# A depthwise convolution on TensorE: from two 64-column tiles with two taps each to four 32-column tiles with four taps each, the shifted inputs made through device memory

## Chip, cores and metric

The kernel runs on the 8 cores of one Trainium2 chip, the same program on each, with no traffic between cores. Each core takes 2048 tokens (a quarter of one of two sequences of 8192) and the 128 tokens before them (the halo). The metric is the device time of the slowest core in microseconds.

## What is computed

One layer of a decoder block with model width 1024. The change concerns the convolution branch alone:

```python
x = x + 0.5 * swiglu(rmsnorm(x), ffn1)                 # width 2816
h = rmsnorm(x)
glu_a, glu_b, q, k, v, g_conv, g_attn = split(h @ w_in)
u = glu_a * sigmoid(glu_b)                             # (B, S, 1024)
u = causal_depthwise_conv(u, w, b)                     # 31 taps: out[t] = sum_k w[k] * u[t - 30 + k]
conv_out = silu(layernorm(u)) @ w_proj
attn_out = sliding_window_gqa(rope(q), rope(k), v) @ w_o   # window 128, 16 heads, 4 kv heads
x = x + (sigmoid(g_conv) * conv_out + sigmoid(g_attn) * attn_out) @ w_out
x = x + 0.5 * swiglu(rmsnorm(x), ffn2)
out = rmsnorm(x)
```

## The kernel before

Activations lie transposed: 128 channels on the partitions, 8 chunks of channels, and a tile of 512 tokens (NT) in the free dimension. A core works through four such tiles, and each tile goes through the whole layer: feed-forward 1 (`ffn_gu`, `ffn_down`), the mixer, feed-forward 2, the final norm. With the first tile the 128 halo tokens go along as far as k, v and u.

Weights don't stay on the chip. Each tile streams all of them again from device memory: they are stored as float32 and cast to bf16 by DMAs that GpSimd issues. Blocks of 128 x 8 x 256 (512 KB in bf16) go through a ring `wa` of 7 slots (stream SA), those of the down projections, 256 KB each, through a ring `wd` of 7 (stream SD). `Stream.next` hands out the next slot and issues the load of the block five places further on in SA's list. That load waits until TensorE has released its slot. The list is recorded in a first dry build, in the order in which the program asks for blocks.

Waits are made by hand-built helpers: `op` and `dma` look up which semaphores the buffers that are read or written depend on, and the engine waits for them before the instruction. The program's order on each engine is the order of these calls. `dma` also waits for the previous transfer on its own semaphore. On SyncE's queue (SP) there are few transfers: the x tile and the positions in, the output out, the constants.

In the mixer `emit_glu(cc)` projects chunk cc of glu_a and glu_b (16 matmuls, L299), ScalarE takes the sigmoid (L501), and VectorE writes the product u to `uT`, which keeps the last 30 tokens of the tile before in its first 30 columns (L503; L545 moves them up after the convolution). Then VectorE makes the shifted input of the convolution: `RR[cc % 2][g2]`, for each half g2 of the chunk's channels, holds the 64 channels on partitions 0 to 63 (L510) and the same channels one token later on partitions 64 to 127 (L512).

`emit_conv(cc)` then contracts over these 128 rows. The stationary matrix of 128 x 64 holds two diagonals, the weights of taps 2j and 2j + 1, and the moving input is `RR` read from column 2j. Sixteen such matmuls (j) for each of the two halves, 32 of 512 columns, sum up 32 taps (the last is zero), the halves going to PSUM partitions 0 to 63 and 64 to 127 (L522). The diagonals come ready-made as a weight block of 128 x 2048 through the same ring (`("W", cc)`, `w2`). Two matmuls with ones (L540, L542) sum the result and its square over the channels for the layer norm, one chunk later. The order is glu(0), then for each cc: glu(cc + 1), conv(cc). After the eight chunks come the query chunks with rotary embedding, the layer norm's arithmetic beside them, and the attention.

Of the kernel before, what the change touches and what calls it, by code (L numbers as in the profile page):

```python
# [88 lines left out]
def dma(q, dsem, out_ap, in_ap, rd=(), wr=()):  # L89
# [9 lines left out]
    for b in rd:  # L99
        b.r[dsem] = dsem.n  # L100

class Stream:
    def __init__(self, q, slots, bufs, sems, keys, src, live=2):
# [10 lines left out]
    def _issue(self):  # L114
        j = self.issued
        if j >= len(self.keys):
            return
        s = j % self.depth
        dma(self.q, self.sems[s], self.slots[s], self.src(self.keys[j]), wr=(self.bufs[s],))
        self.issued += 1  # L120
# [17 lines left out]
def _build(rec):  # L138
    nc = bass.Bass("TRN2", target_bir_lowering=False)
    dt = nc.dram_tensor  # L140
# [5 lines left out]
    cols_d = dt("cols", [128, 9, 8], F32, kind="ExternalInput").ap()  # L146
    w2_d = dt("w2", [8, 128, 2048], F32, kind="ExternalInput").ap()
    misc_d = dt("misc", [128, 16], F32, kind="ExternalInput").ap()
# [7 lines left out]
    with ExitStack() as es:  # L156
# [27 lines left out]
        wd_s = [mksem(f"s_wd{i}") for i in range(ND)]  # L184
        uT = sb("uT", [128, 8, 30 + NT], BF16); uT_b = [Buf() for _ in range(8)]
        RR = [[sb(f"RR{i}{g}", [128, 30 + NT], BF16) for g in range(2)] for i in range(2)]
        RR_b = [[Buf(indep=True) for g in range(2)] for i in range(2)]
        cT = sb("cT", [128, 8, NT], BF16); cT_b = [Buf() for _ in range(8)]
# [69 lines left out]
        def late_setup():  # L258
            cdma(POOL, "ident", ident[:], ident_d, ident_b)
            cdma(POOL, "pswap", pswap[:], pswap_d, pswap_b)  # L260
            cdma(POOL, "masks", masks[:], masks_d, masks_b)
            op(DVE, lambda: nc.vector.memset(onesz[:], 0.0), wr=(onesz_b,))
            op(DVE, lambda: nc.vector.memset(onesz[:, 0, 0:64], 1.0), wr=(onesz_b,))
            op(DVE, lambda: nc.vector.memset(onesz[:, 1, 64:128], 1.0), wr=(onesz_b,))
            allk = [b_ for g_ in kTz_b for b_ in g_]
            op(DVE, lambda: nc.vector.memset(kTz[:], 0.0), wr=allk)
            op(DVE, lambda: nc.vector.memset(vz[:], 0.0), wr=vz_b)
            op(DVE, lambda: nc.vector.memset(uT[:], 0.0), wr=uT_b)
            for i_ in range(2):
                for g_ in range(2):  # L270
                    op(DVE, lambda i_=i_, g_=g_: nc.vector.memset(RR[i_][g_][:], 0.0), wr=(RR_b[i_][g_],))
            for gp in range(2):
                for i in range(4):
                    op(ACT, lambda gp=gp, i=i: nc.scalar.activation(
                        out=sinkt[:, gp, i * 128:(i + 1) * 128], in_=ident[:], func=AF.Exp,
                        bias=misc[:, 2 + gp * 4 + i:3 + gp * 4 + i], scale=0.0),
                       rd=(ident_b, misc_b), wr=(sinkt_b,))
# [174 lines left out]
        def mixer(tile_idx, base, N, full, do_norm=True):  # L452
# [41 lines left out]
            def emit_glu(cc):  # L494
# [10 lines left out]
                if full:  # L505
                    W_ = 30 + N
                    for g2 in range(2):
                        rr, rrb = RR[cc % 2][g2], RR_b[cc % 2][g2]
                        lo, hi = 64 * g2, 64 * g2 + 64
                        op(DVE, lambda: nc.vector.tensor_copy(out=rr[0:64, 0:W_], in_=uT[lo:hi, cc, 0:W_]),  # L510
                           rd=(uT_b[cc],), wr=(rrb,))
                        op(DVE, lambda: nc.vector.tensor_copy(out=rr[64:128, 0:W_ - 1], in_=uT[lo:hi, cc, 1:W_]),  # L512
                           rd=(uT_b[cc],), wr=(rrb,))

            def emit_conv(cc):
                nonlocal pending
# [238 lines left out]
def _pack_shared(inp):  # L755
# [120 lines left out]
```

How the kernel before makes its waits and increments, by code:

```python
    def wait(self, sem, val):  # L34
        if val <= 0:
            return
        if sem is self.sem:
            if val > sem.n or not SAME_ENGINE_SYNC or self.no_self:
                return
        if self.known.get(sem, 0) >= val:
            return
        self.e.wait_ge(sem.h, val)
        self.known[sem] = val
# [31 lines left out]
def op(eng, fn, rd=(), wr=()):  # L75
    for s, v in _deps(rd, wr, eng.sem).items():
        eng.wait(s, v)
    inst = fn()
    eng.sem.n += 1
    inst.then_inc(eng.sem.h, 1)
    ev = eng.sem.n
    for b in wr:
        b.w = {eng.sem: ev}
        b.r = {}
    for b in rd:
        if b.r.get(eng.sem, 0) < ev:
            b.r[eng.sem] = ev
# [1 line left out]
def dma(q, dsem, out_ap, in_ap, rd=(), wr=()):  # L89
    for s, v in _deps(rd, wr, None).items():
        q.wait(s, v)
    q.wait(dsem, dsem.n)
    inst = q.e.dma_start(out=out_ap, in_=in_ap)
    dsem.n += 16
    inst.then_inc(dsem.h, 16)
    for b in wr:
        b.w = {dsem: dsem.n}
        b.r = {}
    for b in rd:
        b.r[dsem] = dsem.n
```

The softmax here doesn't subtract the row's maximum and nothing guards it: scores larger than these inputs give would overflow.

## Time and profile before

| | |
|---|---|
| median of 3 runs | 2008.72 us (1988.82, 2008.72, 2282.69) |
| span of the profiled execution, slowest core | 1984.8 us (cores: 1978.2 to 1984.8) |
| TensorE busy | 1785.2 us, 90% |
| VectorE, ScalarE, GpSimd busy | 663.6, 537.6, 465.6 us |
| moved by DMA, written side | 252.34 MB, mean 127 GB/s |
| read from device memory | 474.46 MB |
| mean granted TensorE clock | 0.963 to 0.968 of 2.4 GHz |

The profile was taken in one execution; its span runs from the first to the last instruction and has no figure of its own for the time around it. The three runs' times are of executions without it. One of them is far from the other two. Times in the rows below are microseconds from the start of that span on its slowest core, unless marked ns.

### The profile page before, as it was taken

What the parts mean: (1) busy time and instruction counts of PE and PEld (TensorE: products, weight loads), DVE (VectorE), ACT (ScalarE), POOL (GpSimd) and SP (SyncE); (2) the same over time, 40 slices, a digit from 0 to 9 for tenths busy, and PEclk for the clock granted to TensorE, in tenths of its full rate; (3) what the DMA queues carried; (4) which work ended last, traced back from release to release, by engine and by line L of the source; (5) the groups of instructions that cost most, each with busy time, mean ns of one, the idle gap of its engine ahead of it and who ended that gap; (6) DMA issues with size and microseconds to landing.
All of it is one profiled execution on the core that took longest, in us unless ns stands there. A gap on an engine that the chain in (4) does not pass through costs nothing.

```text
span 1984.8 us, 25921 instructions; the slowest of 8 cores (1978.2 to 1984.8 us)
## 1 busy us (share of the span) xinstructions
PE 1785.2 (90%) x8762; PEld 804.9 (41%) x8930; DVE 663.6 (33%) x1150; ACT 537.6 (27%) x947; POOL 465.6 (23%) x569
## 2 busy tenths in 40 slices
PE   3899797999999898899999889799999989889997
PEld 1455442434444343343444334243444434334343
DVE  3322445331222246333132234533222124643212
ACT  2111316321221123622221121642122112362211
POOL 2113222112232313121232222211223231312111
PEclk9899898999999999999999989899999999999998
DMA  9899997799999998499999999669999999829987
GB/s 163 103 123 118 136 154 115 83 130 136 136 176 144 146 122 103 78 144 119 145 140 169 143 124 140 101 77 136 129 135 174 145 151 122 105 34 144 119 103 121
DMA packets 398350, 252.34 MB, mean 127 GB/s; under 512 B 9360, under 2 KB 385296, under 8 KB 398224
## 3 DMA queue, kind: packets, MB, share of 16 engines
q0 software_dynamic: 387792, 232.23, 96.1%
q1 hardware_dynamic: 10432, 18.46, 3.2%
q8 instruction: 76, 1.25, 0.3%
q14 instruction: 50, 0.41, 0.1%
HBM read 474.46 MB, written 8.39 MB: 243 GB/s over the span
## 4 chain that ended last, share of the span: by engine, by line
PE 75%; DMA 10%; DVE 6%; issue 4%; ACT 3%; POOL 1%; DVEq 0%; ACTq 0%; POOLq 0%
PE ps L299 45%; PE ps L367 14%; PE ps L522 6%; DMA wa<-wall 5%; DMA wd<-wd 3%; PE ps L667 3%; DMA ident_sb<-ident 2%; PE ps L635 2%; PE ps L639 2%; DVE tmp L647 1%; DVE tmp L429 1%; ACT sq L311 1%; DVE tmp L431 1%; DVE X L576 1%; DVE tmp L645 1%
## 5 line engine op out<-in xcount | busy, mean ns | idle before, releaser
L299 PE MATMUL ps<-xn,wa 128*128 128x512 bf16 x4055 | 943.8, 387 | 52.7 <-DVE xn L322 21.6
L299 PEld LDWEIGHTS ps<-xn,wa 128*128 128x128 bf16 x4160 | 407.6, 99 | 568.4 <-issue 109.3
L93 POOL DMA_DIRECT2D wa<-wall x322 | 282.6, 879 | 1070.7 <-PE ps L299 915.3
L367 PE MATMUL ps<-Hh,wd 128*128 128x512 bf16 x1373 | 318.2, 384 | 15.1 <-DMA wd<-wd 11.3
L343 DVE TENSOR_TENSOR Hh<-ps,tmp 128x512 bf16<-128x512 f32 x176 | 121.4, 691 | 485.8 <-PE ps L299 485.8
L341 ACT ACTIVATE tmp<-ps 128x512 f32<-128x512 f32 x176 | 105.1, 597 | 469.9 <-PE ps L299 469.8
L367 PEld LDWEIGHTS ps<-Hh,wd 128*128 128x128 bf16 x1408 | 136.8, 99 | 176.1 <-issue 27.9
L93 POOL DMA_DIRECT2D wd<-wd x176 | 123.8, 705 | 282.3 <-PE ps L367 282.3
L380 DVE SCALAR_TENSOR_TENSOR X<-ps,X 128x512 f32<-128x512 f32 x64 | 39.8, 684 | 259.2 <-PE ps L367 259.2
L522 PE MATMUL ps<-RR,wa 128*64 128x512 bf16 x1024 | 117.7, 379 | 1.4 <-DVE RR L512 1.4
L311 ACT ACTIVATE sq<-X 128x512 bf16<-128x512 f32 x96 | 54.7, 621 | 169.6 <-PE ps L313 75.1
L322 DVE SCALAR_TENSOR_TENSOR xn<-X,cols_sb,ps 128x512 bf16<-128x512 f32 x96 | 64.3, 742 | 67.1 <-ACT ps L319 67.1
L522 PEld LDWEIGHTS ps<-RR,wa 128*64 128x64 bf16 x1024 | 56.4, 109 | 61.1 <-issue 15.9
L313 PE MATMUL ps<-sq,ones_sb 128*128 128x512 bf16 (+1 forms) x112 | 37.3, 388 | 44.2 <-ACT sq L311 36.1
L621 ACT ACTIVATE PT<-ps 128x512 bf16<-128x512 f32 x128 | 65.7, 597 | 2.6 <-PE ps L618 2.5
L635 PE MATMUL ps<-PT,vz 128*128 128x512 bf16 x124 | 39.5, 397 | 28.5 <-DVE tmp L647 23.4
L613 PE MATMUL ps<-qT,kTz 128*128 128x512 bf16 x128 | 53.5, 418 | 12.3 <-DVE tmp L429 11.2
L667 PE MATMUL ps<-aT,wa 128*128 128x512 bf16 x256 | 60.5, 379 | 0.2
L676 DVE TENSOR_TENSOR tmp<-ps,tmp 128x512 f32<-128x512 f32 x32 | 22.1, 692 | 113.3 <-PE ps L299 105.2
L299 PE MATMUL ps<-cT,wa 128*128 128x512 bf16 x248 | 59.4, 379 | 0.4
L732 ACT ACTIVATE sq<-X 128x512 bf16<-128x512 f32 x32 | 19.4, 630 | 141.8 <-DVE X L380 90.5
L503 DVE TENSOR_TENSOR uT<-ps,tmp 128x512 bf16<-128x512 f32 (+1 forms) x40 | 24.5, 612 | 99.2 <-PE ps L522 74.7
(111 smaller groups left out, 1240.6 us busy)
## 6 DMA issues: line engine op xcount, KB each, us to landing
wa<-wall POOLq DMA_DIRECT2D x322, 512.0 KB, 10.8
wd<-wd POOLq DMA_DIRECT2D x176, 256.0 KB, 6.5
wa<-w POOLq DMA_DIRECT2D x32, 512.0 KB, 8.7
X<-xT SPq DMA_DIRECT2D x4, 2048.0 KB, 16.6
outT<-X SPq DMA_DIRECT2D x8, 1024.0 KB, 9.8
posi<-pos SPq DMA_DIRECT2D x4, 256.0 KB, 13.2
Xh<-xT SPq DMA_DIRECT2D x1, 512.0 KB, 7.0
masks_sb<-masks POOLq DMA_DIRECT2D x1, 384.0 KB, 36.1
```

The costliest lines, as they stand in the source:

```text
L93: inst = q.e.dma_start(out=out_ap, in_=in_ap)
L299: op(PE, lambda kc=kc: nc.tensor.matmul(pst[:, 0:N], lhsT=wslot[:, kc, sub * 128:(sub + 1) * 128], rhs=rhs_t[:, kc, 0:N], start=(kc == 0), ...
L311: op(ACT, lambda c=c, s_t=s_t: nc.scalar.activation(out=s_t[:, 0:N], in_=x_t[:, c, 0:N], func=AF.Square), rd=(x_bufs[c],), wr=(s_b,))
L322: op(DVE, lambda c=c: nc.vector.scalar_tensor_tensor(out=out_t[:, c, 0:N], in0=x_t[:, c, 0:N], scalar=cols[:, gcol, c:c + 1], in1=pst[:, 0:N],
L341: op(ACT, lambda: nc.scalar.activation(out=t_t[:, 0:N], in_=pg[:, 0:N], func=AF.Silu), rd=(pgb,), wr=(t_b,))
L343: op(DVE, lambda: nc.vector.tensor_tensor(out=Hh[:, fc, 0:N], in0=pu[:, 0:N], in1=t_t[:, 0:N], op=ALU.mult), rd=(pub, t_b), wr=(H_b[fc],))
L367: op(PE, lambda pst=pst, dcl=dcl: nc.tensor.matmul(pst[:, 0:N], lhsT=wdt[:, sub, dcl * 128:(dcl + 1) * 128], rhs=Hh[:, fc, 0:N], start=(fc ...
L522: op(PE, lambda j=j, g2=g2: nc.tensor.matmul(pc[64 * g2:64 * g2 + 64, 0:N], lhsT=dg[:, 4 * g2 + j // 4, (j % 4) * 64:(j % 4) * 64 + 64], r ...
L613: op(PE, lambda: nc.tensor.matmul(pst[:, :].rearrange("p (i q) -> p i q", i=4), lhsT=kTz[:, g, slot * 128:(slot + 1) * 128], rhs=qT[:, gp ...
L621: op(ACT, lambda: nc.scalar.activation(out=p_t[:], in_=pst[:, :], func=AF.Exp, scale=0.125), rd=(pb,), wr=(p_b,))
L635: op(PE, lambda: nc.tensor.matmul(pn[:, :], lhsT=vz[:, slot, g * 128:(g + 1) * 128], rhs=p_t[:], start=(e == 0 and n_ == 0), stop=(e == 1 ...
L667: op(PE, lambda hc=hc: nc.tensor.matmul(pao[:, 0:N], lhsT=wpb[:, hc, 128:256], rhs=aT[:, hc, 0:N], start=(hc == 0), stop=(hc == 7)), rd=[w ...
```

## The change

The convolution is cut into four tiles of 32 channels with four taps in each contraction. Partition 32 s + c of the new shifted input holds channel c of a group, s tokens later (s = 0 to 3), for the four groups side by side in the free dimension. A stationary matrix is 128 x 32, four diagonals. Eight steps (j, taps 4j to 4j + 3) for each of four groups make 32 matmuls of 512 columns again, group g going to PSUM partitions 32 g to 32 g + 31. The weight block shrinks from 128 x 2048 to 128 x 1024 and loads into the first half of its slot.

The shifted input is no longer made by VectorE. SyncE stores u of the chunk (128 x 544) to a scratch `ush` in device memory, waits until it has landed, and issues four loads, one for each shift s, of 32 partitions x 4 groups x 540 tokens. There are four such inputs instead of two; they lie in `Hh`, the hidden activations of the feed-forward layers, which are not in use in this stage. The GLU runs three chunks ahead of the convolution instead of one: glu(0), glu(1), glu(2), then glu(cc + 3), conv(cc). `uT` is two columns wider. The clearing of the old `RR` at the start goes.

```diff
+UW = 30 + 512 + 2
+RW = 28 + 512
+NRR = 4
...
+def dma_group(q, dsem, pairs, rd=(), wr=()):
+    for s, v in _deps(rd, wr, None).items():
+        q.wait(s, v)
+    q.wait(dsem, dsem.n)
+    for out_ap, in_ap in pairs:
+        q.e.dma_start(out=out_ap, in_=in_ap).then_inc(dsem.h, 16)
+        dsem.n += 16
+    for b in wr:
+        b.w = {dsem: dsem.n}
+        b.r = {}
+    for b in rd:
+        b.r[dsem] = dsem.n
...
-    w2_d = dt("w2", [8, 128, 2048], F32, kind="ExternalInput").ap()
+    w2_d = dt("w2", [8, 128, 1024], F32, kind="ExternalInput").ap()
+    ush_d = dt("ush", [8, 128, UW], BF16, kind="Internal").ap()
...
-        RR = [[sb(f"RR{i}{g}", [128, 30 + NT], BF16) for g in range(2)] for i in range(2)]
-        RR_b = [[Buf(indep=True) for g in range(2)] for i in range(2)]
+        uT = sb("uT", [128, 8, UW], BF16); uT_b = [Buf() for _ in range(8)]
+        Hflat = Hh[:].rearrange("p a b -> p (a b)")
+        RR = [Hflat[:, 5 * NT * i:5 * NT * i + 4 * RW].rearrange("p (g t) -> p g t", g=4) for i in range(NRR)]
+        RR_b = [H_b[5 * i:5 * i + 5] for i in range(NRR)]
+        RR_s = [mksem(f"s_rr{i}") for i in range(NRR)]
+        ush_b = [Buf() for _ in range(8)]
+        ush_s = [mksem(f"s_ush{i}") for i in range(2)]
...
                 if full:
-                    W_ = 30 + N
-                    for g2 in range(2):
-                        rr, rrb = RR[cc % 2][g2], RR_b[cc % 2][g2]
-                        lo, hi = 64 * g2, 64 * g2 + 64
-                        op(DVE, lambda: nc.vector.tensor_copy(out=rr[0:64, 0:W_], in_=uT[lo:hi, cc, 0:W_]),
-                           rd=(uT_b[cc],), wr=(rrb,))
-                        op(DVE, lambda: nc.vector.tensor_copy(out=rr[64:128, 0:W_ - 1], in_=uT[lo:hi, cc, 1:W_]),
-                           rd=(uT_b[cc],), wr=(rrb,))
+                    dma(SP, ush_s[cc % 2], ush_d[cc], uT[:, cc, :], rd=(uT_b[cc],), wr=(ush_b[cc],))
+                    rr = RR[cc % NRR]
+                    dma_group(SP, RR_s[cc % NRR],
+                              [(rr[32 * s_:32 * s_ + 32, :, :],
+                                ush_d[cc][:, s_:s_ + RW].rearrange("(g c) t -> c g t", g=4)) for s_ in range(4)],
+                              rd=(ush_b[cc],), wr=RR_b[cc % NRR])
...
-                    for j in range(16):
-                        for g2 in range(2):
-                            op(PE, lambda j=j, g2=g2: nc.tensor.matmul(
-                                pc[64 * g2:64 * g2 + 64, 0:N], lhsT=dg[:, 4 * g2 + j // 4, (j % 4) * 64:(j % 4) * 64 + 64],
-                                rhs=RR[cc % 2][g2][:, 2 * j:2 * j + N], start=(j == 0), stop=(j == 15)),
-                               rd=(dgb, RR_b[cc % 2][g2]), wr=(pcb,))
+                    for j in range(8):
+                        for g in range(4):
+                            op(PE, lambda j=j, g=g: nc.tensor.matmul(
+                                pc[32 * g:32 * g + 32, 0:N], lhsT=dg[:, g, j * 32:j * 32 + 32],
+                                rhs=RR[cc % NRR][:, g, 4 * j:4 * j + N], start=(j == 0), stop=(j == 7)),
+                               rd=[dgb] + RR_b[cc % NRR], wr=(pcb,))
...
-            emit_glu(0)
+            AHEAD = 3
+            for cc in range(AHEAD):
+                emit_glu(cc)
             for cc in range(8):
-                if cc + 1 < 8:
-                    emit_glu(cc + 1)
+                if cc + AHEAD < 8:
+                    emit_glu(cc + AHEAD)
                 emit_conv(cc)
```

## Rows read from the trace of the kernel before

**Rows 1.** The page: busy time, then the chain that ended last.

```profile
PE 1785.2 (90%) x8762; PEld 804.9 (41%) x8930; DVE 663.6 (33%) x1150; ACT 537.6 (27%) x947; POOL 465.6 (23%) x569
...
PE 75%; DMA 10%; DVE 6%; issue 4%; ACT 3%; POOL 1%; DVEq 0%; ACTq 0%; POOLq 0%
```

**Rows 2.** Mixer of the second tile, TensorE in order of time (start, length; idle before).

```profile
705.86 6.85 PE L299 MATMUL ps<-xn,wa 128*128 128x512 bf16 x31
...
720.67 3.65 PE L522 MATMUL ps<-RR,wa 128*64 128x512 bf16 x32
724.25 0.39 PE L540 MATMUL ps<-sq,ones_sb 128*128 128x512 bf16 x1
...
724.91 3.40 PE L299 MATMUL ps<-xn,wa 128*128 128x512 bf16 x15
...
762.62 3.64 PE L522 MATMUL ps<-RR,wa 128*64 128x512 bf16 x32
...
768.58 0.38 PE L542 MATMUL ps<-sq,ones_sb 128*128 128x512 bf16 x1
```

**Rows 3.** Groups by line and shape, whole execution.

```profile
L522 PE MATMUL ps<-RR,wa 128*64 128x512 bf16 x1024 | 117.7, 379 | 1.4 <-DVE RR L512 1.4
...
L522 PEld LDWEIGHTS ps<-RR,wa 128*64 128x64 bf16 x1024 | 56.4, 109 | 61.1 <-issue 15.9
...
L512 DVE COPY RR<-uT 64x541 bf16<-64x541 bf16 x64 | 19.2, 300 | 2.1
```

**Rows 4.** Three stretches of the second tile: busy, clock, DMA share, GB/s.

```profile
693.30:698.00 4.70, 4.18 (x8) 0.82 (x9) 4.44 (x7) 0.00 (x0) 0.00 (x0) 0.50 1.09 148
705.90:766.40 60.50, 59.47 (x389) 27.24 (x396) 25.74 (x60) 11.85 (x25) 12.11 (x16) 1.00 1.04 134
766.40:790.00 23.60, 17.28 (x74) 6.94 (x74) 17.92 (x29) 14.55 (x23) 10.19 (x9) 1.00 0.69 85
```

**Rows 5.** DMA, 1050 to 1100 us, feed-forward layer fed as fast as DMA gives.

```profile
DMA packets 13935, 7.53 MB, mean 151 GB/s; under 512 B 245, under 2 KB 13621, under 8 KB 13932
```

**Rows 6.** DMA, 706 to 766 us, the stage of the change.

```profile
wa<-wall POOLq DMA_DIRECT2D x10, 512.0 KB, 7.0
```

**Rows 7.** SyncE's queue in order of time, start to end.

```profile
1.06 0.39 SPq L93 DMA_DIRECT2D cols_sb<-cols  x1
1.50 0.42 SPq L93 DMA_DIRECT2D misc_sb<-misc  x1
...
568.54 3.01 SPq L93 DMA_DIRECT2D outT<-X  x2
571.64 0.68 SPq L93 DMA_DIRECT2D posi<-pos  x1
```

**Rows 8.** DMA, 560 to 600 us, both kinds of queue busy.

```profile
q1 hardware_dynamic: 1200, 2.36, 18.2%
...
outT<-X SPq DMA_DIRECT2D x2, 1024.0 KB, 9.3
...
posi<-pos SPq DMA_DIRECT2D x1, 256.0 KB, 14.0
```

**Rows 9.** DMA, 1970 to 1985 us, stores alone.

```profile
q1 hardware_dynamic: 1056, 2.10, 37.5%
...
outT<-X SPq DMA_DIRECT2D x2, 1024.0 KB, 4.4
```

**Rows 10.** DMA, 145 to 155 us, one load beside weights.

```profile
posi<-pos SPq DMA_DIRECT2D x1, 256.0 KB, 2.8
```

**Rows 11.** All engines, 709 to 712 us: first GLU chunk.

```profile
709.34 1.28 ACT L501 ACT_TABLE_LOAD   x1 [2.79 <-PE ps L299]
...
711.34 0.69 DVE L503 TENSOR_TENSOR uT<-ps,tmp 128x512 bf16<-128x512 f32 x1 [4.18 <-ACT tmp L501]
```

**Rows 12.** TensorE, 149 to 152 us: four short matmuls, then four long.

```profile
150.20 0.39 PE L373 MATMUL ps<-Hhh,wd 128*128 128x128 bf16 x4
150.43 0.81 PE L367 MATMUL ps<-Hh,wd 128*128 128x512 bf16 x3
```

More of the change, by code:

```diff
@@ L118, in _issue @@
         s = j % self.depth
-        dma(self.q, self.sems[s], self.slots[s], self.src(self.keys[j]), wr=(self.bufs[s],))
+        src = self.src(self.keys[j])
+        dst = self.slots[s] if src.shape[1] == self.slots[s].shape[1] else self.slots[s][:, 0:src.shape[1]]
+        dma(self.q, self.sems[s], dst, src, wr=(self.bufs[s],))
         self.issued += 1
@@ L184, in _build @@
         wd_s = [mksem(f"s_wd{i}") for i in range(ND)]
-        uT = sb("uT", [128, 8, 30 + NT], BF16); uT_b = [Buf() for _ in range(8)]
-        RR = [[sb(f"RR{i}{g}", [128, 30 + NT], BF16) for g in range(2)] for i in range(2)]
-        RR_b = [[Buf(indep=True) for g in range(2)] for i in range(2)]
+        uT = sb("uT", [128, 8, UW], BF16); uT_b = [Buf() for _ in range(8)]
[5 more added lines that the diff above has]
+        ush_s = [mksem(f"s_ush{i}") for i in range(2)]
         cT = sb("cT", [128, 8, NT], BF16); cT_b = [Buf() for _ in range(8)]
@@ L268, in late_setup @@
             op(DVE, lambda: nc.vector.memset(uT[:], 0.0), wr=uT_b)
-            for i_ in range(2):
-                for g_ in range(2):
-                    op(DVE, lambda i_=i_, g_=g_: nc.vector.memset(RR[i_][g_][:], 0.0), wr=(RR_b[i_][g_],))
             for gp in range(2):
@@ L287, in asrc @@
             if key[0] == "W":
-                return w2_d[key[1]].rearrange("p (a b) -> p a b", a=8)
+                return w2_d[key[1]].rearrange("p (a b) -> p a b", a=4)
             return ablk(key[1])
@@ L812, in _pack_shared @@
     dw[:CW] = np.asarray(inp["conv_dw_w"][0], f)
-    dw = dw.reshape(16, 2, 8, 2, 64)
-    w2 = np.zeros((8, 2, 64, 2, 16, 64), f)
-    ii = np.arange(64)
+    dw = dw.reshape(8, 4, 8, 4, 32)
+    w2 = np.zeros((8, 4, 32, 4, 8, 32), f)
+    ii = np.arange(32)
     w2[:, :, ii, :, :, ii] = dw.transpose(4, 2, 1, 3, 0)
-    w2 = np.ascontiguousarray(w2.reshape(8, 128, 2048))
+    w2 = np.ascontiguousarray(w2.reshape(8, 128, 1024))
     misc = np.zeros((128, 16), f)
```

## The prediction

> **What bounds the kernel now.** Read the page first: TensorE is busy nine tenths of the span and carries three quarters of the chain that ended last, DMA a tenth of it [rows 1]. Then look only at the stage that is changed, in order of time: the eight GLU chunks with their convolutions, 705.86 to about 768.9 us in the second tile. TensorE has no hole there worth naming: a chunk's cycle is 7.57 us (720.67 to 728.24), made of 3.58 us of convolution, 0.53 us of two statistics matmuls, and the rest GLU projection [rows 2]. The table by stretch says the same: 59.5 of 60.5 us busy at full clock [rows 4]. So TensorE bounds this stage. The DMA stands just behind it: its share is 1.04 and it moves 134 GB/s there [rows 4], and where a feed-forward layer draws weights as fast as it can it gives 151 GB/s with the share at its top [rows 5]. A weight block lands 7.0 us after issue in the stage [rows 6]. The stage comes four times, once a tile.
>
> **What the change removes.** (a) Half of the convolution's streaming. Now 32 matmuls go in pairs of 64-column tiles: 3.58 us / 16 = 224 ns a pair, and the two weight loads of a pair lie inside it (109 ns each) [rows 2, 3]. Afterwards there are 8 groups of four 32-column tiles. If four run side by side as two do, a chunk costs 8 x 0.224 = 1.8 us. Can TensorE issue that fast? Four matmuls of 128 columns with their loads take 0.23 us, until the next line starts [rows 12], 57 ns each, and four of these are 228 ns, hardly above 224. So 1.83 us, bounded above by 3.6 (no gain from four tiles). The saving is 1.75 us a chunk, 56 us in all if nothing else came last. The row for 64 columns against the tiling rule of the Trainium skill (TensorE: Matmul & The Clock Gate, "Measured speedup vs the span model"): it gives 3.07 times for four row tiles, not 4; by that figure a group would be about 281 ns and a chunk 2.25 us, an estimate from that page; in the sum only the last chunk of a tile would feel it, 0.4 us each. No row here shows four tiles. (b) 128 copies on VectorE, 38 us at 0.30 us each [rows 3]; they stood on the path only before the first convolution of a tile, 0.5 us, so I cost their going at that, and it is swallowed below. (c) Half of each convolution weight block, 256 of 512 KB, eight a tile.
>
> **What it adds.** Per chunk, on SyncE's queue: one store to device memory of 128 rows of 1088 bytes (136 KB), a wait until it has landed, then four loads of 135 KB, each 128 runs of 1080 bytes, and only then the next chunk's store. Behind that wait stand the four loads and every later chunk; the convolution waits for the last load. 676 KB go this way per chunk, against 256 KB saved.
>
> The price of a hop comes from three groups of rows. Alone, 1056 packets of mostly 2 KB took 37.5% of 15 us = 5.6 us; over 16 engines that is 66 packets each, 85 ns a packet. A 1 MB store landed in 4.4 us; 64 to 66 packets in 2 stores, so 33 x 85 ns = 2.8 us each, which leaves 1.6 us fixed per hop [rows 9]. A 256 KB load beside light weight traffic landed in 2.8 us, in keeping with that [rows 10]. In competition, 2.36 MB in 1200 packets went from 568.54 until 14.0 us after 571.64 [rows 7, 8]: 17.1 us, less 1.6 fixed is 15.5, over 75 packets an engine 207 ns each. So the competing weights add 122 ns to a packet of 85. A run of 1080 bytes then costs 45 ns alone, 109 ns if competition scales with bytes, 167 ns if it is paid per packet. Each engine has 8 packets of store and 32 of loads per chunk. SyncE issues one transfer every 0.44 us (1.06 to 1.50) [rows 7], so four take 1.8 us.
>
> **The bounce's period**, from one chunk's loads to the next chunk's: the next store queues behind the loads on the same ring, so all 40 packets and one fixed time of 1.6 us are in series.
> - alone: issue-bound, 1.8 + 1.6 + 0.36 = 3.8 us
> - by bytes: 1.6 + 40 x 0.109 = 6.0 us
> - by packets: 1.6 + 40 x 0.167 = 8.3 us
>
> TensorE's own cycle would be 7.57 - 1.75 = 5.8 us. The competition is real: weights ask for 768 KB per 5.8 us = 135 GB/s of a rate of about 151 [rows 5], and the bounce comes on top. I take 7.0 us, between the two contended prices, for the first five steps, and 4.8 us for the last two, when the GLU blocks are through and less competes. This is where I chose, and the result hangs on it.
>
> **The sum for one tile.** u of chunk 0 is written at 711.34 + 0.69 = 712.0 us [rows 11]. Store: 1.6 + 1.1; loads: 1.6 + 4.4 (mid prices). Chunk 0's shifted input is there at 720.7, when TensorE, three chunks ahead, has just finished four GLU chunks (705.86 + 4 x 3.46 = 719.7): the lookahead pays for the first latency. From there the bounce's chain is the slower one: 720.7 + 5 x 7.0 + 2 x 4.8 = 765.3 us for chunk 7. Now its convolution starts at 762.62 [rows 2]; afterwards 2.7 us later. Chunks 5 to 7 have no GLU work left to put between them, so TensorE is busy about 2.3 us in each 5 to 7; after the thin work of a norm its clock is granted at 0.50, that is 1.2 GHz [rows 4], and I expect it here: the last convolution takes 3.6 us (no shorter than before), and the first query chunk and the statistics up to 2.1 us more, of which I take 1.5. Loss: 2.7 + 1.5 = 4.2 us a tile, 17 us for four. The weights themselves I cost at nothing: the bounce takes about half the DMA while it is active, the five blocks in flight ahead (2.6 MB, some 17 us of supply) cover the stage, and the query stage behind it draws only a share of 0.69 [rows 4]. If that cover is gone, TensorE waits on weights too, a few us in the first tile above all. Query and attention stages only shift.
>
> **The reference time.** The profiled span is 1984.8 us; the fastest run is 1988.8, so some 4 us lie around it. The three runs' median is 2008.7, but one of the three was 2282.7; the other two have a mean of 1998.8, and I count from there: 1998.8 + 17 = 2016 us.
>
> **Rivals.**
> 1. The bounce is quick (alone price): then TensorE leads. Its last GLU ends at 705.86 + 8 x 3.46 + 4 x 1.83 + 3 x 0.44 = 742.2, u is written 1.5 us later, the bounce takes 2.0 + 3.3, so chunk 7 can start at 749.0, 13.6 us earlier, and saves 1.8 more in itself: 15.4 x 4 = 61 us, 1938 us. For it: stores alone landed in 4.4 us per MB [rows 9], and one load beside weights in 2.8 us [rows 10]. Against it: a weight block is almost always in flight here [rows 4, 6]. A milder form, in which the period just equals TensorE's 5.8, gives 720.7 + 40.3 = 761.0 and a full clock: -3.4 x 4 = -14 us, 1985.
> 2. The wait on SyncE's chain is paid per packet: first input at 712.0 + 1.6 + 1.3 + 1.6 + 5.3 = 721.8, then 5 x 8.3 + 2 x 6.0 = 775.3, 12.7 later, and 2 of clock: 14.7 x 4 = +59 us, 2058, slower. It decides from a period of about 7.9 us on, where the loss passes 2%. For it: the 122 ns added per packet of 2 KB [rows 8, 9] when neighbours were 512-byte runs. The Trainium skill (DMA: Bandwidth & Descriptors, "Queues, rings and completion order") says each engine takes turns between its queues packet by packet, which speaks for this price.
> 3. Four tiles do not overlap better than two: the convolution stays at 3.6 us, TensorE leads again with its 7.57 us cycle, u of chunk 7 comes at about 751, its input at 760, and the stage ends within 3 us of now: 1999 to 2011.
>
> **How the numbers follow.** Forecast case (period 6.2 to 7.8) 0.45; rival 1 quick 0.14, its mild form 0.10; rival 2 0.26; rival 3 0.05. A measurement of this kernel can tell about 2% from no change, 40 us. Faster by more needs rival 1: 0.14. Slower by more is most of rival 2 and the upper edge of the forecast with weights late as well: 0.30. Within: 0.56. The range takes in mild rival 1 and most of rival 2, with the runs' own 20 us of spread: 1962 to 2060.
>
> **What would show it.** L522 with 1024 matmuls again in groups of four with cycle about 0.224 us (right) or 0.44 (rival 3). TensorE's holes before the convolutions, ended by the DMA of the shifted input, growing from chunk 1 on, with the last two widest; the start-to-start of chunks 1 to 5 near 7 us. Granted clock below 1.00 at the stage's end. On SyncE the wait for the store's landing 2.5 to 3.5 us; loads landing 5 to 7. VectorE 38 us lighter. I am wrong if the holes are ended by weight blocks (then the DMA's total work counts, not the chain's latency), or if the stage ends before 760 us after an unchanged start.

## The result and the profile after

The changed kernel took 2083.99 us (median of 4 runs, 2071.48 to 2091.54), against 2010.17 for the kernel before. The ratio is 1.0414, 95% interval 1.0326 to 1.0502: 4% slower, some 83 us by the ratio, where 2016 us was forecast. One run of the kernel before, 2282.69 us, and a few others below lie far above the rest of their kernel; the ratios are made without such runs.

The page of the kernel after, its busy times and its chain (against [rows 1]):

```profile
PE 1796.3 (86%) x8930; PEld 789.4 (38%) x8930; DVE 622.2 (30%) x1018; ACT 540.1 (26%) x947; POOL 465.8 (22%) x569
...
PE 68%; DMA 16%; DVE 6%; issue 4%; ACT 3%; SPq 3%; DVEq 0%; ACTq 0%; POOL 0%; POOLq 0%
PE ps L319 44%; PE ps L387 13%; DMA ush<-uT 5%; DMA Hh<-ush 4%; DMA wd<-wd 3%; PE ps L687 3%; SPq L110 2%; DMA wa<-wall 2%; PE ps L655 2%; PE ps L659 1%; PE ps L540 1%; DMA X<-xT 1%; PE ps L333 1%; DVE tmp L449 1%; DVE tmp L667 1%
```

TensorE is as busy as before in microseconds, although half the convolution's streaming is gone (part of its work now runs at half clock, see below), and the chain has moved: DMA 16% instead of 10%, with the store (ush<-uT, 5%) and the loads (Hh<-ush, 4%) as lines of their own and SyncE's issuing (SPq) 3%. The two queues of the page, the convolution's groups, and the transfers with their median landing:

```profile
q0 software_dynamic: 387792, 223.84, 87.0%
q1 hardware_dynamic: 33472, 40.62, 7.3%
...
L540 PE MATMUL ps<-Hh,wa 128*32 128x512 bf16 x1024 | 89.8, 513 | 115.6 <-DMA Hh<-ush 114.5
...
Hh<-ush SPq DMA_DIRECT2D x128, 135.0 KB, 5.0
...
ush<-uT SPq DMA_DIRECT2D x32, 136.0 KB, 5.8
```

Bytes went up by 13.8 MB (252.34 to 266.14), the count of weight packets (q0) is the same. The new row is the convolution's idle time: 115.6 us before L540, nearly all of it ended by the landing of the shifted input. Now the same stage in order of time, the second tile, TensorE alone (start, length; idle before). Before, it ran from 705.86 to 766.3 us, 60.4 us, with no hole worth naming [rows 2]:

```profile
749.05 13.98 PE L319 MATMUL ps<-xn,wa 128*128 128x512 bf16 x64
769.46 3.61 PE L540 MATMUL ps<-Hh,wa 128*32 128x512 bf16 x32 [6.44 <-DMA Hh<-ush]
773.00 4.68 PE L319 MATMUL ps<-xn,wa 128*128 128x512 bf16 x16
...
784.96 1.91 PE L540 MATMUL ps<-Hh,wa 128*32 128x512 bf16 x32 [1.45 <-DMA Hh<-ush]
...
792.73 1.91 PE L540 MATMUL ps<-Hh,wa 128*32 128x512 bf16 x32 [1.86 <-DMA Hh<-ush]
...
800.91 1.91 PE L540 MATMUL ps<-Hh,wa 128*32 128x512 bf16 x32 [2.28 <-DMA Hh<-ush]
...
810.29 3.61 PE L540 MATMUL ps<-Hh,wa 128*32 128x512 bf16 x32 [6.94 <-DMA Hh<-ush]
...
817.04 3.60 PE L540 MATMUL ps<-Hh,wa 128*32 128x512 bf16 x32 [2.17 <-DMA Hh<-ush]
...
824.36 3.60 PE L540 MATMUL ps<-Hh,wa 128*32 128x512 bf16 x32 [2.75 <-DMA Hh<-ush]
```

The stage takes 749.05 to 827.9 us, 78.9. TensorE's account of it: eight GLU chunks of 3.46 us 27.7, eight convolutions of 1.84 us 14.7, seven pairs of statistics 3.1, holes 6.4 + 1.5 + 1.9 + 2.3 + 6.9 + 2.2 + 2.8 = 24, and the rest, 9.4 us, for work at half clock: convolutions of 3.60 us instead of 1.84, a GLU chunk in 4.68 instead of 3.5. The convolutions saved 13.9 us and the small gaps of the old order another 1; the holes and the clock took 33. The stage is 18.5 us longer, 74 us in four such tiles, and the first tile is worse than this one (below). Who set the holes is on SyncE's queue, the same tile (the four loads of a chunk are one row):

```profile
755.50 0.34 SPq L96 DMA_DIRECT2D ush<-uT  x1
760.45 2.03 SPq L110 DMA_DIRECT2D Hh<-ush  x4
762.58 0.88 SPq L96 DMA_DIRECT2D ush<-uT  x1
770.85 1.72 SPq L110 DMA_DIRECT2D Hh<-ush  x4
...
776.74 1.72 SPq L110 DMA_DIRECT2D Hh<-ush  x4
...
801.42 2.02 SPq L110 DMA_DIRECT2D Hh<-ush  x4
...
810.92 1.72 SPq L110 DMA_DIRECT2D Hh<-ush  x4
...
817.28 2.00 SPq L110 DMA_DIRECT2D Hh<-ush  x4
```

Read down the rows of four loads. From 760.45 to 817.28 are seven periods, 8.1 us each on average, and they swing between 5.9 (770.85 to 776.74) and 10.4 (760.45 to 770.85). The store of chunk 1 is issued at 762.58 and its loads at 770.85: 8.3 us for one hop. On the eight cores the mean period is 8.4 to 9.7 us in the first tile and 7.8 to 8.7 in the others, 8.4 over all, and a store's loads go out 6.0 to 6.4 us behind it on average. In every period SyncE issues the next store at once, 0.1 us (at most 0.5) behind the last load: u is there long before, and this chain waits for nothing but its own landings.

### The profile page after: what moved, and what is told of

Read it like the earlier page. It is cut to its first block, busy times and chain, and to the rows that moved or that the text cites. A ratio compares the mean times of both kernels' runs of the same rounds, so it can differ in the third digit from the quotient of the medians.

```text
span 2090.5 us, 26262 instructions; the slowest of 8 cores (2052.7 to 2090.5 us)
## 1 busy us (share of the span) xinstructions
PE 1796.3 (86%) x8930; PEld 789.4 (38%) x8930; DVE 622.2 (30%) x1018; ACT 540.1 (26%) x947; POOL 465.8 (22%) x569
## 2 busy tenths in 40 slices
DMA packets 421393, 266.14 MB, mean 127 GB/s; under 512 B 11920, under 2 KB 408336, under 8 KB 421264
## 4 chain that ended last, share of the span: by engine, by line
PE 68%; DMA 16%; DVE 6%; issue 4%; ACT 3%; SPq 3%; DVEq 0%; ACTq 0%; POOL 0%; POOLq 0%
PE ps L319 44%; PE ps L387 13%; DMA ush<-uT 5%; DMA Hh<-ush 4%; DMA wd<-wd 3%; PE ps L687 3%; SPq L110 2%; DMA wa<-wall 2%; PE ps L655 2%; PE ps L659 1%; PE ps L540 1%; DMA X<-xT 1%; PE ps L333 1%; DVE tmp L449 1%; DVE tmp L667 1%
## 5 line engine op out<-in xcount | busy, mean ns | idle before, releaser
L319 PE MATMUL ps<-xn,wa 128*128 128x512 bf16 x4160 | 968.5, 391 | 40.2 <-DVE xn L342 21.3
L387 PE MATMUL ps<-Hh,wd 128*128 128x512 bf16 x1408 | 319.9, 384 | 13.9 <-DMA wd<-wd 11.9
L540 PE MATMUL ps<-Hh,wa 128*32 128x512 bf16 x1024 | 89.8, 513 | 115.6 <-DMA Hh<-ush 114.5
L540 PEld LDWEIGHTS ps<-Hh,wa 128*32 128x32 bf16 x1024 | 34.1, 120 | 166.8 <-issue 157.0
L342 DVE SCALAR_TENSOR_TENSOR xn<-X,cols_sb,ps 128x512 bf16<-128x512 f32 x96 | 64.3, 743 | 68.7 <-ACT ps L339 68.7
L547 DVE TENSOR_SCALAR X<-ps,cols_sb 128x512 f32<-128x512 f32 x32 | 24.0, 751 | 169.0 <-PE ps L540 169.0
L319 PE MATMUL ps<-qT,wa 128*128 128x512 bf16 x256 | 56.5, 379 | 1.2 <-DVE qT L700 1.2
```

Of the source, the lines that this page charges most:

```text
L319: op(PE, lambda kc=kc: nc.tensor.matmul(pst[:, 0:N], lhsT=wslot[:, kc, sub * 128:(sub + 1) * 128], rhs=rhs_t[:, kc, 0:N], start=(kc == 0), ...
L342: op(DVE, lambda c=c: nc.vector.scalar_tensor_tensor(out=out_t[:, c, 0:N], in0=x_t[:, c, 0:N], scalar=cols[:, gcol, c:c + 1], in1=pst[:, 0:N],
L387: op(PE, lambda pst=pst, dcl=dcl: nc.tensor.matmul(pst[:, 0:N], lhsT=wdt[:, sub, dcl * 128:(dcl + 1) * 128], rhs=Hh[:, fc, 0:N], start=(fc ...
L540: op(PE, lambda j=j, g=g: nc.tensor.matmul(pc[32 * g:32 * g + 32, 0:N], lhsT=dg[:, g, j * 32:j * 32 + 32], rhs=RR[cc % NRR][:, g, 4 * j:4 ...
```

## The experiments

Each kernel is the changed one with the edit shown. Where a theory is named A, B or C, A is: the chain of one chunk after the other on SyncE sets the period; B: the hops are dear through competition or latency, on whatever queue; C: the added traffic delays the weights. The expected bands are in microseconds, and the kernel before, measured again beside each group of runs, had medians of 1987 to 2010 us; so small differences are read from the ratios.

**Stores from ScalarE's queue (e1).**

```diff
-                    dma(SP, ush_s[cc % 2], ush_d[cc], uT[:, cc, :], rd=(uT_b[cc],), wr=(ush_b[cc],))
+                    dma(ACT, ush_s[cc % 2], ush_d[cc], uT[:, cc, :], rd=(uT_b[cc],), wr=(ush_b[cc],))
```

> The changed kernel with the stores of u issued from ScalarE's queue, the loads still from SyncE's. Theory A (the chain of one chunk after the other on SyncE, each store queued behind the loads before it, sets the period of 8.1 us): stores no longer stand behind loads, the period falls to about 6 us, some 14 us less a tile, 2025 to 2045 us. Rival B (competition with the weight stream and the latency of the hops themselves set it, whatever the queue): period still 7.5 or more, 2065 to 2090 us. Rival C (the DMAs' total work delays the weights): no change, and TensorE's holes end at weight blocks.

Measured 2047.32 us, ratio 1.0249 (1.0224 to 1.0274) against 1.0414: 2 us above A's band, 18 below B's. TensorE in the second tile:

```profile
753.58 3.61 PE L540 MATMUL ps<-Hh,wa 128*32 128x512 bf16 x32 [7.33 <-DMA Hh<-ush]
...
761.39 1.91 PE L540 MATMUL ps<-Hh,wa 128*32 128x512 bf16 x32
...
767.22 1.91 PE L540 MATMUL ps<-Hh,wa 128*32 128x512 bf16 x32
...
788.25 3.60 PE L540 MATMUL ps<-Hh,wa 128*32 128x512 bf16 x32 [6.92 <-DMA Hh<-ush]
...
793.27 1.91 PE L540 MATMUL ps<-Hh,wa 128*32 128x512 bf16 x32 [0.45 <-DMA Hh<-ush]
...
799.10 3.21 PE L540 MATMUL ps<-Hh,wa 128*32 128x512 bf16 x32 [3.38 <-DMA Hh<-ush]
```

From 761.39 on four convolutions come every 5.83 us: TensorE leads, the throughput of the bounce is enough once a store needn't stand behind the loads before it, though single landings are no quicker (median 7.0 us for a store and 7.3 for a load, against 5.8 and 5.0). What is left are the holes at both ends: 7.3 us before the first, and 6.9, 0.5 and 3.4 behind the last GLU chunk, where a bounce's latency has nothing in front of it. The serial order cost about 1.6%. This run is still 5.5% above the one without a bounce that follows (ratio 0.9700), and the holes at the two ends with their half clock (3.61, 4.34 and 3.60 us where 1.84 and 3.5 are the rule) are what its trace shows for that.

**No bounce (e2).** The convolution reads a buffer `RRo` that is filled once.

```diff
-                    dma(SP, ush_s[cc % 2], ush_d[cc], uT[:, cc, :], ...)
-                    dma_group(SP, RR_s[cc % NRR], ...)
-                                rhs=RR[cc % NRR][:, g, 4 * j:4 * j + N], start=(j == 0), stop=(j == 7)),
+                                rhs=RRo[0][:, g, 4 * j:4 * j + N], start=(j == 0), stop=(j == 7)),
```

> The changed kernel without the store and the four loads; the convolution reads a buffer that is filled once, so its output isn't the convolution of u. Shows what the four-tile convolution and the lookahead are worth alone. If four tiles run side by side (0.22 us a group) and nothing else came last: 2005 less 56 to 61, 1940 to 1955 us. If the order (three chunks ahead) or the weights cost something: 1965 or more. If TensorE gains nothing from four tiles: about 2005.

Measured 1938.94 us, ratio 0.9700 (0.9674 to 0.9727). The row of its convolution, all tiles (count | busy, mean ns of one | idle before):

```profile
L537 PE MATMUL ps<-RRo,wa 128*32 128x512 bf16 x1024 | 61.1, 380 | 0.0
```

61.1 us busy over 32 chunks, and in the trace a chunk's 32 matmuls take 1.84 us (712.03 to 713.87), 0.23 us a group of four. So the tiling, the halved weight block and the lookahead together are worth 3%, some 60 us, against the 56 that the prediction put on the streaming. All of the loss is the bounce.

**Bounce made, convolution doesn't read it (e3, then e6).** As e2, but store and loads stay.

> As the run without a bounce (the convolution reads a buffer filled once, so its output isn't the convolution of u), but the store and the four loads are all made, and nobody waits for them except the next use of their buffers. Theory A and B (the wait for the landing costs, not the traffic): within 10 us of the run without a bounce. Rival C (40 MB more DMA traffic delays the weights): 25 us or more above it, with holes on TensorE that end at weight blocks.

Measured 2070.54 us, ratio 1.0367 (1.0341 to 1.0393). The time is as far above e2 as C asked, but C's sign is missing: TensorE's holes in the stage ended at the statistics' inputs, not at weight blocks. The kernel had a waiter that I hadn't seen. The widest hole, and the wait of the stage with the largest total (total us, times, longest):

```profile
786.92 0.59 PE L560 MATMUL ps<-sq,ones_sb 128*128 128x512 bf16 x1 [8.32 <-DVE sq L553]
...
ACT uT L565 <- DMA ush<-uT: 39.2, 6, 8.9
```

After each convolution ScalarE copies the last 30 columns of `uT` to its front (L545 before, L565 here). That overwrites what the store reads, so ScalarE waits for the store's landing, with the next sigmoid and the squares for the statistics queued behind it. In e6 these copies go behind the mixer's gates:

```diff
-                op(ACT, lambda: nc.scalar.activation(out=uT[:, cc, 0:30], in_=uT[:, cc, N:N + 30], func=AF.Copy), ...)
+                if not full:
+                    op(ACT, lambda: nc.scalar.activation(out=uT[:, cc, 0:30], in_=uT[:, cc, N:N + 30], func=AF.Copy), ...)
...
+            for cc in range(8):
+                op(ACT, lambda cc=cc: nc.scalar.activation(out=uT[:, cc, 0:30], in_=uT[:, cc, N:N + 30], func=AF.Copy), ...)
             for j in range(4):
                 wo, wob = SA.next(("A", 52 + j))
```

> As the run with a bounce that the convolution doesn't read (its output isn't the convolution of u), with one more change: the copy of the last 30 columns of u, which has to wait until the store has read u, goes behind the gates of the mixer, so that ScalarE doesn't stand in it during the stage. Theory A (the waits for landing cost, not the traffic): within 10 us of the run without a bounce, 1939 to 1950. Rival C (the traffic delays the weights): 1960 or more, with holes that end at weight blocks.

Measured 1946.99 us, ratio 0.9752 (0.9734 to 0.9771), 0.5% or some 10 us above e2 and in the band of A. So the bounce's traffic beside the weights (22 MB; the 40 expected for e3 were too many) costs little by itself; theory C falls. SyncE's queue in that run shows something else:

```profile
719.65 0.39 SPq L96 DMA_DIRECT2D ush<-uT  x1
731.93 1.72 SPq L110 DMA_DIRECT2D Hh<-ush  x4
...
740.89 2.33 SPq L110 DMA_DIRECT2D Hh<-ush  x4
```

Here TensorE doesn't wait in the stage, the weights flow at full pace, and the same chain is slower: 12.3 us from one store to its loads (719.65 to 731.93), mean periods of 10.8 to 12.0 by tile and core, 11.4 over all. In the changed kernel TensorE's holes hold back the weight stream, which fits its bounce being quicker than this; e7 and e12 try that.

**Competition taken away (e7, e12).** The GLU and convolution blocks are loaded in part; in e12 also the query blocks and six gate blocks.

```diff
             if key[0] == "W":
-                return w2_d[key[1]].rearrange("p (a b) -> p a b", a=4)
+                return w2_d[key[1]].rearrange("p (a b) -> p a b", a=4)[:, 0:1, :]
+            if 28 <= key[1] < 36:          # in e12: 24 <= key[1] < 42
+                return ablk(key[1])[:, 0:1, :]
             return ablk(key[1])
```

> The changed kernel with the weights of the GLU blocks and of the convolution loaded in part only (1 of 8 and 1 of 4 slices; the rest of the slot is stale, so the output isn't the reference's). The bounce is whole. If competition with the weight stream sets the price of a hop: the period falls from 8 us to 4 to 5, TensorE leads, 1940 to 1970 us. If the hops are slow by themselves (write to device memory, read back, four issues): period 7 or more, 2050 to 2080.

Measured 2012.41 us, ratio 1.0091 (1.0069 to 1.0114), between the bands. The periods of the second tile explain it:

```profile
719.25 1.78 SPq L110 DMA_DIRECT2D Hh<-ush  x4
...
725.02 1.73 SPq L110 DMA_DIRECT2D Hh<-ush  x4
...
730.24 3.01 SPq L110 DMA_DIRECT2D Hh<-ush  x4
...
743.12 2.23 SPq L110 DMA_DIRECT2D Hh<-ush  x4
...
753.56 2.37 SPq L110 DMA_DIRECT2D Hh<-ush  x4
...
763.91 1.73 SPq L110 DMA_DIRECT2D Hh<-ush  x4
```

5.8 and 5.2 us for the first two, then 12.9 for two, and then 10.4 and 10.4. From chunk 4 on the ring, five blocks ahead, fetches the whole query and gate blocks, and the DMA's share says so:

```profile
717.30:735.00 17.70, 17.68 (x130) 7.68 (x128) 5.12 (x8) 3.88 (x8) 3.17 (x6) 1.00 0.67 136
...
745.00:765.00 20.00, 8.95 (x67) 3.29 (x68) 3.00 (x5) 2.09 (x5) 2.57 (x3) 0.79 1.17 174
```

It is 0.67 in the first part and 1.17 from 745 us on (the column before the last), with the same transfers on SyncE. With those blocks light too:

> As the run with light GLU and convolution weights, and the query blocks and the first six gate blocks, which are in flight during the second half of the stage, are loaded in part too (1 of 8 slices; stale elsewhere, so the output isn't the reference's). If competition with the weight stream is the whole of what the sum missed: the late periods of 10 us fall to the early ones of 5 to 6 of that run, TensorE leads or nearly so, 1950 to 1975 us. If the chain is slow by itself from some chunk on: periods of 7 and more remain in the second half, 1995 or more.

Measured 1968.81 us, ratio 0.9844 (0.9760 to 0.9927), in the band. The first two stores of the second tile and their loads:

```profile
721.02 0.34 SPq L96 DMA_DIRECT2D ush<-uT  x1
722.94 1.99 SPq L110 DMA_DIRECT2D Hh<-ush  x4
725.02 0.38 SPq L96 DMA_DIRECT2D ush<-uT  x1
728.63 1.73 SPq L110 DMA_DIRECT2D Hh<-ush  x4
```

Mean periods in every tile and core lie at 5.3 to 6.1 us, and a store's loads go out 3.3 to 3.5 us behind it. So the mean period over all cores and tiles, 8.4 us in the changed kernel, becomes 7.0 and 5.7 as weights are taken out from beside the chain, and 11.4 where they flow freely (e6). The first store of a tile has no loads of this chain before it, and by it the two parts of the price come apart. Its loads go out 5.7 us behind it in the changed kernel and 2.0 here (means over cores and tiles): that is the weight stream. From 2.0 for the first store to 3.6 for the later ones here: that is standing behind the loads of the chunk before.

**By what measure is competition paid (e8, e10).** e8 loads the same bytes in runs of 2160, e10 cuts each run of 1080 to 540.

```diff
-                              [(rr[32 * s_:32 * s_ + 32, :, :],
-                                ush_d[cc][:, s_:s_ + RW].rearrange("(g c) t -> c g t", g=4)) for s_ in range(4)],
+# e8                           [(rr[32 * s_:32 * s_ + 32, :, :].rearrange("p (h r) t -> p h (r t)", h=2),
+#                                ush_d[cc].rearrange("(c h r) t -> c h (r t)", c=32, h=2)[:, :, s_:s_ + 2 * RW]) for s_ in range(4)],
+# e10                          [(rr[32 * s_:32 * s_ + 32, :, 0:RW // 2],
+#                                ush_d[cc][:, s_:s_ + RW // 2].rearrange("(g c) t -> c g t", g=4)) for s_ in range(4)],
```

> The changed kernel with the same bytes loaded from the scratch in half as many runs, of 2160 bytes instead of 1080 (they hold other channels than the convolution needs, so the output isn't the reference's). If competition is paid per packet: 16 packets fewer an engine and chunk, 16 x 0.12 = 2 us less a period, 8 us or more a tile, 2040 to 2055 us. If it is paid per byte, or the latency of the hops sets the period: 2070 to 2090.

> The changed kernel with each run of the four loads half as long, 540 bytes; the rest of the shifted input is stale, so the output isn't the reference's. As many transfers and runs, 270 KB a chunk less. If the bytes of the bounce set the period (109 ns a run of 1080 bytes beside the weights): 32 x 0.05 = 1.7 us less a period, 2040 to 2050 us. If a hop's landing is a wait that depends on the weight stream and hardly on its own size: 2065 to 2085, periods still about 8 us.

e8: 2092.84 us, ratio 1.0505 (1.0480 to 1.0529), mean periods 7.8 to 9.5. A store's loads go out 5.9 us behind it instead of 6.2, where the price per packet asked for 2 us less; and four loads take 2.6 us to issue instead of 2.0, which eats even that. So the price isn't paid per run of the bounce. e10: ratio 1.0333 (1.0227 to 1.0439, from two runs, 2042.89 and 2070.42 us), which overlaps the changed kernel's interval, so the time decides nothing. Its periods are clearer: 6.8 to 8.2, mean 7.5 against 8.4. Half the bytes of the loads give 0.9 us, half of what the price by bytes asked for. The number of runs explains nothing of the period, their bytes a part, and most of it isn't explained by either.

**One hop on the chip (e11).** 16 transfers a chunk straight from `uT` to the shifted input, 12 on SyncE, 4 on ScalarE.

```diff
+                    pr_ = [(rr[32 * s_:32 * s_ + 32, g, :], uT[32 * g:32 * g + 32, cc, s_:s_ + RW]) for g in range(4) for s_ in range(4)]
...
+                    for q_, sm, sel in ((SP, RR_s[cc % NRR], pr_[0:12]), (ACT, RA_s[cc % NRR], pr_[12:16])):
...
+                            q_.e.dma_start(out=o_, in_=i_).then_inc(sm.h, 16)
```

> The shifted input fetched from u on the chip in one hop: 16 transfers of 32 partitions x 1080 bytes a chunk, straight from uT, 12 from SyncE's queue and 4 from ScalarE's, no scratch and no wait between transfers. Issue is then 12 x 0.44 = 5.3 us a chunk, under TensorE's 5.8. If the two landings one behind the other are what costs: steady chunks at 5.8 us, holes only before the first and behind the last GLU, 1985 to 2010 us. If transfers beside the weight stream are slow in themselves (bytes, engines): 2040 or more.

Measured 2077.24 us, ratio 1.0418 (1.0350 to 1.0487): the time of two hops, in the band for slow transfers. The reason is another, one I had priced wrongly. SyncE's queue in the second tile:

```profile
729.13 68.69 SPq L537 DMA_DIRECT2D Hh<-uT  x96
```

96 issues in 68.7 us, 0.72 us each instead of 0.44: 8.6 us a chunk. Such a row would also join issues with pauses between them, but here there are none: one issue takes 0.51 to 1.78 us, 0.59 in the median, and SyncE waited for u four times in all, once a tile. The issue of 12 transfers is the bound here. Whether one hop would be cheap with less to issue stays open.

**Shifted input by copies (e4, e5).** 16 copies of 32 partitions a chunk, 10 on VectorE, 6 on ScalarE, two chunks ahead, no scratch. In e4 both engines' copies were booked on the same buffers as `op` does it, in e5 each waits only for u and for the buffer's last reader (`before`).

```diff
+                    for g in range(4):
+                        for s_ in range(4):
+                            o_ = rr[32 * s_:32 * s_ + 32, g, :]
+                            i_ = uT[32 * g:32 * g + 32, cc, s_:s_ + RW]
+                            if (4 * g + s_) % 8 in (2, 5, 7):
+                                cop(ACT, before, lambda: nc.scalar.activation(out=o_, in_=i_, func=AF.Copy), rd=(uT_b[cc],), wr=RR_b[cc % NRR])
+                            else:
+                                cop(DVE, before, lambda: nc.vector.tensor_copy(out=o_, in_=i_), rd=(uT_b[cc],), wr=RR_b[cc % NRR])
```

> The four-tile convolution, but the shifted input made on the chip: 16 copies of 32 partitions x 540 a chunk, 10 on VectorE and 6 on ScalarE, no scratch, two chunks ahead. VectorE then has 10 x 0.30 + 2.06 = 5.1 us of work in TensorE's cycle of 5.8, ScalarE 6 x 0.65 + 1.44 = 5.3. If both keep up: 1950 to 1965 us. If the copies become the bound (0.45 us each or more on either engine): a cycle of 6.5 or more, 1975 to 2010 us.

> The copies of the last such run, with one thing mended: there each copy waited for the last copy of the other engine (all were booked on the same buffers), so 16 copies of 0.31 and 0.65 us ran in a row. Now both engines only wait for u and for the last reader of the buffer, and copy side by side: VectorE 10 x 0.31 + 2.06 = 5.2 us a chunk, ScalarE 6 x 0.65 + 1.44 = 5.3, in TensorE's cycle of 5.8. If that holds: 1940 to 1965 us (the run without a bounce had 1939). If either engine falls behind because its other work arrives in the middle of the copies: cycle 6.5 to 7.5, 1975 to 2010.

e4: ratio 1.0655 (1.0621 to 1.0688; two runs, 2126.71 and 2129.07 us), above both bands: the two engines took turns, 16 copies in a row. e5: 1994.74 us, ratio 0.9997 (0.9986 to 1.0007), in the second band. Its steady chunks do run at TensorE's 5.83 us, not at the 6.5 or more that came with the second band; what it loses stands at the start and the end. VectorE in e5:

```profile
722.21 0.69 DVE L536 TENSOR_TENSOR uT<-ps,tmp 128x512 bf16<-128x512 f32 x1 [1.55 <-ACT tmp L534]
723.00 3.47 DVE L550 COPY Hh<-uT 32x540 bf16<-32x540 bf16 x10
...
732.04 0.75 DVE L566 TENSOR_SCALAR X<-ps,cols_sb 128x512 f32<-128x512 f32 x1
```

Before a tile's first sigmoid stands a table load of 1.28 us, and its second one waits on ScalarE behind six copies of 4.0 us. Then u and ten copies take VectorE 4.3 us a chunk and leave little to catch up with: the result of convolution 0, done at 723.5, is read from PSUM at 732.04, and TensorE stands 4.4 us at chunk 0's statistics.

**Fewer, larger copies (e9, e13).** Bring the groups to partitions 0 to 31, then shift within the buffer: partitions 32 to 63 from them in one copy, 64 to 127 from 0 to 63 in one copy on each engine.

```diff
+                    for g in range(4):
+                        o_, i_ = rr[0:32, g, :], uT[32 * g:32 * g + 32, cc, :]
+                        # g 0, 1 on VectorE, g 2, 3 on ScalarE
...
+                    cop(DVE, before, lambda: nc.vector.tensor_copy(out=rr[32:64, :, 0:UW - 1], in_=rr[0:32, :, 1:UW]), wr=wb)
...
+                    cop(DVE, before, lambda: nc.vector.tensor_copy(out=rr[64:128, 0:2, 0:UW - 2], in_=rr[0:64, 0:2, 2:UW]), wr=wb)
+                    cop(ACT, before, lambda: nc.scalar.activation(out=rr[64:128, 2:4, 0:UW - 2], in_=rr[0:64, 2:4, 2:UW], func=AF.Copy), wr=wb)
```

> The four-tile convolution with the shifted input made on the chip in 8 instructions a chunk instead of 16: four copies of 32 partitions bring the groups to partitions 0 to 31 (2 on VectorE, 2 on ScalarE), one copy of all four groups writes partitions 32 to 63 from them one token on, one copy of 64 partitions for two groups on VectorE and one on ScalarE writes 64 to 127 two tokens on. VectorE 2 x 0.31 + 1.1 + 0.6 + 2.1 = 4.4 us a chunk, ScalarE 2 x 0.65 + 1.1 + 1.45 = 3.9, both under TensorE's 5.8. If the copies' occupancy is what kept the 16-copy kernel at the time of the kernel before (backlog from the first chunk on, statistics late): 1940 to 1960 us. If it is the latency behind the last GLU chunk (some 5 us) or the half clock after it: 1965 to 1985.

Measured 1956.51 us, ratio 0.9838 (0.9777 to 0.9899), in the first band: 1.6% less than the kernel before, whose interval doesn't reach to no change but doesn't clear 2% either, and well below the changed kernel (1.0414). The copies, by group:

```profile
L547 ACT ACTIVATE Hh<-uT 32x544 bf16<-32x544 bf16 x64 | 41.8, 654 | 29.6 <-DVE uT L536 28.8
...
L558 ACT ACTIVATE Hh<-Hh 64x1084 bf16<-64x1084 bf16 x32 | 35.4, 1105 | 33.0 <-DVE Hh L553 33.0
...
L553 DVE COPY Hh<-Hh 32x2172 bf16<-32x2172 bf16 x32 | 24.7, 771 | 24.7 <-ACT Hh L547 24.7
...
L549 DVE COPY Hh<-uT 32x544 bf16<-32x544 bf16 x64 | 20.2, 316 | 4.3
...
L557 DVE COPY Hh<-Hh 64x1084 bf16<-64x1084 bf16 x32 | 15.5, 484 | 3.3
```

VectorE's share is 0.63 + 0.77 + 0.48 = 1.9 us a chunk instead of 3.1: a copy of 2172 elements takes 0.77 us where four of 544 take 1.26. TensorE still stands 3.6 us behind convolution 1, at chunk 0's statistics. e13 puts the statistics two chunks behind:

```diff
-                    for f_ in pending:
-                        f_()
-                    pending = []
+                    if len(pending) == 2:
+                        pending.pop(0)()
```

> The on-chip copies in 8 instructions, with the statistics matmuls two chunks behind the convolution instead of one. If TensorE's hole of 3.6 us behind chunk 1 (waiting for VectorE's cast) and the half clock after it are what is left above the run without a bounce (1939): 1940 to 1952 us. If the copies only push the wait elsewhere: 1955 or more.

Measured 1970.93 us, ratio 0.9856 (0.9771 to 0.9941): no different from e9, in the second band. The hole behind convolution 1 is gone, and others of 2.9 and 2.4 us stand before convolutions 6 and 7, where PSUM banks wait for VectorE:

```profile
742.84 2.49 PE L567 MATMUL ps<-Hh,wa 128*32 128x512 bf16 x32 [2.89 <-DVE X L573]
...
748.73 3.60 PE L567 MATMUL ps<-Hh,wa 128*32 128x512 bf16 x32 [2.43 <-DVE X L573]
```

## Why the prediction was wrong

The place and the mechanism were as forecast, a chain on SyncE that TensorE waits for, and so was the sign; the size was not. By its own steps:

- *TensorE bounds the stage, DMA stands just behind.* Right (e2: 3% without the bounce).
- *Four tiles run side by side, 1.83 us a chunk.* Right: 1.84. Neither 2.25, the estimate from 3.07 times, nor 3.6 was seen. A group of four costs 0.23 us.
- *The period, "I take 7.0 us ... and 4.8 us for the last two".* This is the step that failed. Measured in the tile shown: 8.2 for the first five, 9.5 and 6.4 for the last two; over all cores and tiles 8.4. Of its parts, issuing (four loads, 2.0 us) and the landing of the loads (5.0 us in the median) were as forecast; the wait for the store's landing was put at 2.5 to 3.5 us and took 6.2. Two terms of that were too small. The uncontended price, 3.8, left out that the store stands behind the loads before it even when little else moves: by the prediction's own 45 ns a run these are 32 x 0.045 = 1.4 us, and with light weights the later stores took 1.6 us more than the first, and the period was 5.7. The contended price was scaled from a queue of large transfers that drained without pause [rows 8]. The chain is made of waits for single landings, and the first store of a tile, with none of them before it, already took 5.7 us against the 2.7 of the sum, and 2.0 where the weights were light. The period follows the weights beside it: 5.7, 7.0, 8.4 and 11.4 us in e12, e7, the changed kernel and e6. Rival 2's number, 8.3, is the one that came out, but not its reason: by packets e8 should have gained 2 us a period and gained nothing. Nor did the turn-taking that it cites speak for a price per run: the Trainium skill (DMA: Bandwidth & Descriptors, "Queues, rings and completion order") lets an engine drain a whole packet of many descriptors before it turns, and the rows count single runs.
- *The first latency.* 8.7 us was forecast from u to its input. Store at 755.50, loads complete at 769.3: 13.9. The lookahead of three chunks didn't pay for it, a hole of 6.4 us remained.
- *The clock.* The level was right (1.2 GHz at the end: the granted clock was 0.56 from 803 to 829 us), the amount not: 1.5 us plus the last convolution, against 9.4 us, because the three last convolutions, their statistics and the first convolution with the GLU chunk behind it ran at half clock.
- *The weights at nothing.* Right within some 10 us, by e6.
- *What would show it.* The holes didn't grow towards the end: the two widest stand before convolution 0 (6.4 us) and convolution 5 (6.9), the first behind the last GLU chunk.
- A waiter was missing: ScalarE's copy of the last columns waits for the store (e3). In the changed kernel it costs nothing (40 copies waited 0.2 us in all), because ScalarE comes to it only behind a convolution that has itself waited for loads issued after that store had landed.

Added up for the second tile: chunk 7's convolution was forecast to start 59.4 us after the stage's start and started 75.3 after it (824.36 - 749.05). 5.6 us of the difference are the first input, 10.3 the seven steps behind it. Four times 15.9 are 64 us, and with the 17 of the sum 81 of the 83 measured. The clock isn't in that: the last convolution starts when its input lands, whatever the ones before it took, so most of the 9.4 us lies where TensorE would have waited anyway.

Not settled: what in the DMA makes a single landing wait on the weight stream. Half as many runs gave nothing, half the bytes of the loads 0.9 us.

## What to carry to other kernels

Price a chain of transfer, wait, transfer by the landing of a single transfer with the other streams at full pace, not by a queue's throughput; and remember that the stream slows when the consumer waits, so the measured chain flatters itself. A lookahead pays for a latency only in the middle (e1): count what it costs before the first and behind the last item, and what the work there takes if the clock has fallen. Here, where data only had to be shifted across partitions, a few large copies on the chip (e9) beat the trip through memory by 5 to 6%.

## What was not expected of the hardware

- Beside the full weight stream (e6) it took 7.9 to 9.4 us, by tile and core, from the issue of a store of 136 KB to that of its loads, against 3.4 with most of the weights beside it gone (e12), though the kernel lost only 0.5% by this traffic.
- Issues on SyncE cost 0.72 us each in a row of 96 transfers of 34 KB, against 0.44 at the start of the kernel.
- Copies in bf16 on VectorE: 316 ns for 32 partitions x 544 elements, 771 for 32 x 2172. By these two that is 0.28 ns an element of the row and 0.16 us a copy, which gives 0.47 us for 64 x 1084 (measured 0.484): twice the partitions cost next to nothing. ScalarE needs 654 and 1105 ns for rows of 544 and 1084.
